# A hybrid decoder step on one core: another order of the attention units, and the first chunk of the next projection ahead of each attention's last value product

## The chip, the core and the metric

The kernel runs on one core of one Trainium2 chip. The metric is the device time of one execution in microseconds; the median of three runs is quoted. The profile is one further execution, recorded by the hardware profiler; its span runs from the first to the last recorded instruction.

## The reference, cut

One layer of a decoder trunk over 1024 prompt rows and 8 sample rows. Every group of heads gets its columns from one input projection; four groups are mixed, gated, projected back and added to the input.

```python
hn = rms_norm(x, g_n)
p = hn @ w_in                      # q, k, v, gates, pool input, z: 31 tiles of 128 columns
o_a = fox_attention(...)           # 4 heads, causal, cumulative log-forget bias
o_b = nsa_attention(...)           # gate0*compressed + gate1*selected blocks + gate2*sliding window
o_c = pool_mix(...)                # trailing means, one linear map for each channel group
o_m = mem_attention(q, mem_kv)     # 4 heads into 256 memory tokens
y = x + (concat(o_a, o_b, o_c, o_m) * silu(z)) @ w_out
y = rms_norm(y, final_g)
...
```

Each attention is a masked softmax of scores times values. The 8 sample rows read their past keys and values from paged caches; `cache_nsa_kv` is one of them.

## The kernel before, in words

**Projections.** The weights are taken in 31 tiles of 128 columns (TILES). A tile is multiplied in three chunks of 344 rows, and a chunk is 8 blocks of the contraction by 3 passes (high by high, low by high, high by low parts; lines 551 to 553, in `passes`), 24 matmuls. `project(m)` does the three chunks of tile m, `chunk(n)` (L584) the single chunk n % 3 of tile n // 3, so chunk 27 is the first chunk of tile 9. POOL splits each weight tile into its two parts (`split`, L1982 and L1984), and SP loads it.

**Attention units.** All attention is cut into 56 units, `attention_units` (L80): what, the pair of heads j, the block i of 128 queries, the first block of keys and the number nk of key blocks of 128. Units 0 to 7 are the memory attention (nk 4), 8 to 23 FoX (FOX_0 = 8; nk = i + 1), 24 to 55 the selected and window branches of NSA (NSA_0 = 24). Before, FoX takes its units in pairs of both j with nk 4, 4, 8, 8, 7, 7, 6, 6, 5, 5, 3, 3, 2, 2, 1, 1; NSA four units of 4, then by falling length 8, 8, 7, 7, 6, 6, ten of 5, and four each of 3, 2 and 1. A unit is wide if nk > 4. WIN_U is the first window unit of full length (5 blocks); there DVE makes the window table (L1548, L1549).

**One unit on the engines.** PE makes scores (`scores`, L667), DVE their negative maxima (`negmax`, L1507) and ACT the exponentials. PE turns the probabilities P by transposes (`turn_p`, L683, into three banks: the fourth piece waits until the first is copied out); ACT copies the even pieces (L1133) and DVE the odd ones (L1561). PE multiplies the turned P with the values (`weigh_v`, L704) and transposes the sums (L708), and DVE multiplies the result by the reciprocal sums into the output (`norm`, L1538 for memory and FoX, L1542 for NSA). In NSA, POOL adds the part to the output (L2071). For FoX, POOL adds the causal mask to the last block of the unit's forget table (L2056). The loop on PE is `attend(u0, u1)` (L711): for each u it issues scores(u), weigh_v(u - 2), turn_p(u - 1). weigh_v waits for the copies of that unit's turned P and for the multiply of the unit before (semaphore s_on). At its end, attend waits for s_on to reach u1, for the last multiply.

**The order of the work.** A list written by hand, STEPS (L109), sets one order of steps for PE, ACT and DVE. attend 0 is memory, attend 1 FoX, attend 2 NSA; behind each stand projection steps. `gates` (L804) are matmuls of 16 columns. `pair_job` (L741, step "pair") turns one pair of pages of `cache_nsa_kv`, which SP loads in its own order (`load_pair`, L2126, four transfers for a pair); from the thirteenth load on (q = 12, the first for pair 6) they stand behind

```python
if q == 12:
    sp.wait_ge(s_on, PHASE[0][1])    # 8: the last multiply of the memory attention
```

Of the kernel before, what the change touches and what calls it, by code (L numbers as in the profile page):

```python
# [79 lines left out]
def attention_units():  # L80

    mem = [("mem", j, i2, 0, 4) for i2 in range(NQ // 2) for j in range(2)]
    fox = [("fox", j, i, 0, i + 1) for i in (3, 7, 6, 5, 4, 2, 1, 0) for j in range(2)]
    nsa = [("sel", j, i, 0, i + 1) for i in range(NQ) for j in range(2)]
    nsa += [("win", j, i, max(0, i - WIN_T), min(i, WIN_T) + 1) for i in range(NQ) for j in range(2)]
    return mem, fox, sorted(nsa, key=lambda u: (u[4] != 4, -u[4]))


MEM_U, FOX_U, NSA_U = attention_units()
UNITS = MEM_U + FOX_U + NSA_U  # L90

WIN_U = next(u for u in range(len(UNITS)) if UNITS[u][0] == "win" and UNITS[u][2] >= WIN_T)
NSA_0 = len(MEM_U) + len(FOX_U)
# [7 lines left out]
def groups(u):  # L101
# [11 lines left out]
         ("project", 5), ("natural", 4), ("take", 5), ("project", 6), ("pair", 4), ("pair", 5), ("take", 6),  # L113
         ("project", 7), ("natural", 6), ("take", 7), ("first", 0), ("natural", 7), ("project", 8), ("take", 8),
         ("attend", 0),
         ("chunk", 27), ("gates", 0), ("pair", 6), ("chunk", 28), ("chunk", 29), ("take", 9),
         ("chunk", 30), ("natural", 9), ("forget", 0), ("forget", 1), ("chunk", 31), ("chunk", 32), ("take", 10),
         ("chunk", 33), ("natural", 10), ("chunk", 34), ("chunk", 35), ("take", 11),
         ("chunk", 36), ("first", 1), ("pair", 7), ("chunk", 37), ("chunk", 38), ("take", 12), ("attend", 1),
         ("project", 13), ("natural", 2), ("natural", 5), ("take", 13), ("gather", 0),  # L120
         ("project", 14), ("natural", 13), ("take", 14),
         ("project", 15), ("take", 15), ("compress", 0), ("pair", 8), ("pair", 9), ("gather", 1),
         ("project", 16), ("pair", 10), ("pair", 11), ("natural", 15), ("take", 16),
# [3 lines left out]
         ("project", 19), ("cmp_turn", 0), ("take", 19),  # L127
         ("chunk", 60), ("natural", 19), ("cmp_out", 0), ("chunk", 61), ("first", 2), ("cmp_out", 1), ("chunk", 62),
         ("take", 20), ("attend", 2),
         ("project", 21), ("natural", 20), ("take", 21), ("pool_mean", 0),  # L130
         ("project", 22), ("take", 22), ("pool_mean", 1),
         ("project", 23), ("pool_last", 0), ("pool_map", 0), ("take", 23),
         ("project", 24), ("take", 24), ("sample_new", 0),
# [38 lines left out]
def build(nc, x_p, x_s, c_fox, c_lf, c_nsa, st_win, st_pool, c_mem, ptab, mem_p, norm_g, w_in, b_f, pe_, w1,  # L172
# [3 lines left out]
    with ExitStack() as ctx:  # L176
# [328 lines left out]
        def _(pe):  # L505
# [140 lines left out]
            def scores(u):  # L646
                what, j, i, k0, nk = UNITS[u]
                done = u - 2 if nk <= 4 and u and UNITS[u - 1][4] <= 4 else u - 1
                if done >= 0 and UNITS[done][0] == "mem":
                    pe.wait_ge(s_P, 2 * (done + 1))  # L650
                elif done >= 0:
                    pe.wait_ge(s_nm, 2 * (done + 1))
                q, k = AUG[:, Q_AT[what] + j, :], AUG[:, K_AT[what] + j, :]
                if what == "mem":
                    for a in range(2):
                        for e in range(2):
                            r = slice(e * DH, (e + 1) * DH)
                            last = mm(bk(score_bank(u, e))[:, a * NMEM:(a + 1) * NMEM],
                                      q[r, (2 * i + a) * P:(2 * i + a + 1) * P], k[r, 0:NMEM], start=True, stop=True)
                    last.then_inc(s_S, 1)  # L660
                    return
                masks = {nk - 1: m_diag} if what == "fox" and i == 3 else {}
                parts = [(c, min(4, nk - c), e) for c in range(0, nk, 4) for e in range(2)]
                inside = {c: [b for b in masks if c <= b < c + 4] for c in range(0, nk, 4)}
                for c, n, e in parts:
                    r = slice(e * DH, (e + 1) * DH)
                    last = mm(bk(score_bank(u, e) + c // 4)[:, 0:n * P], q[r, i * P:(i + 1) * P],  # L667
                              k[r, (k0 + c) * P:(k0 + c + n) * P], start=True, stop=not inside[c])
                for c, n, e in parts:
                    for b in inside[c]:  # L670
                        last = mm(bk(score_bank(u, e) + c // 4)[:, (b - c) * P:(b - c + 1) * P], identb[:, :],
                                  masks[b][:, :], start=False, stop=(b == inside[c][-1]))
                last.then_inc(s_S, 1)
# [12 lines left out]
            def weigh_v(u):  # L686
                what, j, i, k0, nk = UNITS[u]
                pe.wait_ge(s_cA, even(G0[u + 1]))
                pe.wait_ge(s_cD, odd(G0[u + 1]))
                if u:  # L690
                    pe.wait_ge(s_on, u)
                wide = 2 if what == "mem" else 1
                for b in range(2 if what == "mem" else nk):
                    for e in range(2):
                        h, t = 2 * j + e, k0 + b
                        v = {"fox": nat[:, t, 256 + h * DH:256 + (h + 1) * DH],
                             "mem": nat[:, t, 256 + h * DH:256 + (h + 1) * DH],
                             "sel": nat[:, t, 384 + j * DH:384 + (j + 1) * DH],
                             "win": vw[:, t, j * DH:(j + 1) * DH]}[what]
                        if what == "mem":  # L700
                            p_ = turned_p(u, e, 0, 4).rearrange("p (a t c) -> p t a c", a=2, t=2)[:, b]
                        else:
                            p_ = turned_p(u, e, b, 1)
                        mm(bk(7)[e * DH:(e + 1) * DH, 0:wide * P], v, p_, start=(b == 0),  # L704
                           stop=(b == (1 if what == "mem" else nk - 1)))
                pe.wait_ge(s_rb, u + 1)
                for a in range(wide):
                    last = tr(bk(7)[:, (2 + a) * P:(3 + a) * P], sums_at(u)[0][:, a * P:(a + 1) * P], ident[:, :])  # L708
                last.then_inc(s_pv, 1)

            def attend(u0, u1):  # L711

                jobs_taken()
                turn_p(u0)
                if u0 == 0:
                    taken(8)
                elif u0 == FOX_0:
                    taken(12)
                scores(u0 + 1)
                if u0 == NSA_0:  # L720
                    taken(20)
                for u in range(u0 + 2, u1 + 2):
                    if u < u1:
                        scores(u)
                    weigh_v(u - 2)
                    if u - 1 < u1:
                        turn_p(u - 1)

                pe.wait_ge(s_on, u1)
                pe.wait_ge(s_cA, even(G0[u1]))  # L730
                pe.wait_ge(s_cD, odd(G0[u1]))
# [1229 lines left out]
        def _(pool):  # L1961
# [84 lines left out]
            pool.wait_ge(s_aug, 64)  # L2046
            for u in range(FOX_0 + 2, NSA_0):
                _, j, i, _, _ = UNITS[u]
                if u == FOX_0 + 4:
                    pool.wait_ge(s_proj, 13)  # L2050
                    split(0, 16 * 8, WH[:, 0, :, :], WL[:, 0, :, :], 15)
                if u >= FOX_0 + 4:
                    pool.wait_ge(s_nm, 2 * (u - 1))
                for e in range(2):
                    last_block = FORGET[2 * j + e][:, i * P:(i + 1) * P]
                    g.tensor_tensor(last_block, last_block, m_diag[:, :], ALU.add).then_inc(s_fm, 1)  # L2056
# [345 lines left out]
```

## Time and profile before

| what | us |
|---|---|
| median of three runs | 820.71 (818.95 to 821.31) |
| the profiled execution | 821.78 |
| its span | 820.0 |
| PE busy | 768.3 (94%) |
| VectorE (DVE) busy | 378.9 (46%) |
| ScalarE (ACT) busy | 282.2 (34%) |
| GpSimd (POOL) busy | 170.3 (21%) |

The rows below come from the profiled execution. A page part counts the whole span. A timeline lists one engine's instructions in order, runs of equal ones as one row with their count; what stands in brackets is the time that the engine idled ahead of the row, and the instruction that ended it. A windows view gives busy time inside a stretch, and the clock granted to TensorE as a share of full speed. PEld is the weight load of TensorE, SPq is SP's DMA queue. Some matmuls in f32 count twice in the trace: the four value products of a memory unit stand there as x8.

### The profile page before, as it was taken

To read this page: it belongs to the slowest core of one execution; us is meant where nothing else is said; L and a number is where in the kernel's file an instruction comes from. 1 tells how busy PE (TensorE), PEld (TensorE's weight loads), DVE (VectorE), ACT (ScalarE), POOL (GpSimd) and SP (SyncE) were. 2 spreads that over 40 slices of the span, in tenths; PEclk is the share of its full clock that TensorE was granted. 3 is DMA by queue.
4 is the path that set the end of the run, shared out by engine and by line. 5 is a ranking of instruction groups with operands and counts; after the bars stand their busy time and mean duration, and the time that the engine had idled before them with its cause. 6 is when DMAs were issued, how large, how long until landed. Compare 5 with 4: busy or idle time off the path is not lost.

```text
span 820.0 us, 15201 instructions
## 1 busy us (share of the span) xinstructions
PE 768.3 (94%) x5664; PEld 644.7 (79%) x5664; DVE 378.9 (46%) x828; ACT 282.2 (34%) x638; POOL 170.3 (21%) x164
## 2 busy tenths in 40 slices
PE   2999998998998999999989999899999999999996
PEld 2899866996777999999857776599988888777773
DVE  4742363425762301313467877738731126624334
ACT  6522363223672202311246766502122225312111
POOL 4146640242120420320220111225222220000000
PEclk9999999999999999999999999999999999999999
DMA  8523300353303455121500000003425567465621
GB/s 269 145 72 98 80 2 14 70 155 106 155 1 120 151 144 169 51 69 46 168 3 2 2 1 2 2 18 79 116 75 163 174 199 217 142 207 172 183 81 55
DMA packets 101880, 81.52 MB, mean 99 GB/s; under 512 B 10013, under 2 KB 95276, under 8 KB 101736
## 3 DMA queue, kind: packets, MB, share of 16 engines
q1 hardware_dynamic: 100352, 79.74, 32.2%
q10 hardware_dynamic: 1456, 0.82, 0.5%
q8 instruction: 45, 0.74, 0.4%
q14 instruction: 27, 0.22, 0.1%
HBM read 70.91 MB, written 13.87 MB: 103 GB/s over the span
## 4 chain that ended last, share of the span: by engine, by line
PE 81%; DVE 5%; SPq 4%; issue 4%; ACT 3%; DMA 2%; POOL 2%; POOLq 0%; DVEq 0%; ACTq 0%
PE PS L551 15%; PE PS L553 15%; PE PS L552 15%; PE PS L704 7%; PE PS L683 6%; PE PS L667 5%; PE PS L767 4%; PE PS L899 2%; SPq L2126 2%; PE PS L987 2%; PE PS L708 2%; SPq L2109 1%; DMA OB<-in_x_prompt 1%; POOL WL L1984 1%; PE PS L741 1%
## 5 line engine op out<-in xcount | busy, mean ns | idle before, releaser
L551 PE MATMUL PS<-HH,WH 128*128 128x344 f32 (+1 forms) x752 | 258.6, 344 | 6.8 <-issue 1.8
L553 PE MATMUL PS<-HH,WL 128*128 128x344 f32 (+1 forms) x752 | 252.7, 336 | 0.0
L552 PE MATMUL PS<-HL,WH 128*128 128x344 f32 (+1 forms) x752 | 252.6, 336 | 0.0
L551 PEld LDWEIGHTS PS<-HH,WH 128*128 128x128 f32 x752 | 143.8, 191 | 20.0 <-issue 7.0
L552 PEld LDWEIGHTS PS<-HL,WH 128*128 128x128 f32 x752 | 143.9, 191 | 5.9 <-issue 0.5
L553 PEld LDWEIGHTS PS<-HH,WL 128*128 128x128 f32 x752 | 143.8, 191 | 5.7
L1982 POOL TENSOR_TENSOR WH<-WR,onesc 128x1024 fp32r<-128x1024 f32 x31 | 60.9, 1965 | 343.8 <-PE PS L553 215.5
L1240 ACT ACTIVATE PP<-PP,stat 128x640 f32<-128x640 f32 (+7 forms) x96 | 70.8, 739 | 31.3 <-DVE stat L1507 31.3
L1984 POOL TENSOR_TENSOR WL<-WR,WH 128x1024 fp32r<-128x1024 f32 x31 | 76.6, 2471 | 2.4
L683 PE MATMUL PS<-ident,PP 128*128 128x128 f32 x472 | 65.6, 278 | 2.5 <-ACT AUG L1133 0.8
L667 PE MATMUL PS<-AUG 64*128 64x512 f32 (+3 forms) x288 | 57.6, 505 | 3.7 <-DVE stat L1507 2.0
L1561 DVE COPY AUG<-PS 128x256 f32<-128x256 f32 (+3 forms) x80 | 41.9, 524 | 40.9 <-PE PS L683 40.5
L683 PEld LDWEIGHTS PS<-ident,PP 128*128 128x128 f32 x472 | 53.7, 142 | 7.3 <-ACT AUG L1133 5.3
L704 PE MATMUL PS<-AUG,NAT 128*64 128x128 f32 (+1 forms) x640 | 47.2, 289 | 8.9 <-DVE OB L1538 5.1
L704 PEld LDWEIGHTS PS<-AUG,NAT 128*64 128x64 f32 x640 | 35.7, 136 | 24.8 <-ACT AUG L1133 13.3
L1133 ACT ACTIVATE AUG<-PS 128x384 f32<-128x384 f32 (+4 forms) x88 | 47.1, 539 | 5.4 <-PE PS L683 4.0
L1133 ACT ACTIVATE NAT<-PS 128x512 f32<-128x512 f32 (+1 forms) x37 | 20.8, 563 | 75.2 <-PE PS L643 27.0
L667 PEld LDWEIGHTS PS<-AUG 64*128 64x128 f32 x288 | 24.0, 187 | 24.2 <-issue 18.6
L1386 ACT ACTIVATE WR<-PP 128x1024 f32<-128x1024 f32 (+1 forms) x9 | 9.5, 1058 | 87.1 <-DVE PP L1949 79.9
L1822 DVE COPY NAT<-PS 128x512 f32<-128x512 f32 x16 | 11.1, 692 | 57.8 <-PE PS L899 57.6
L2071 POOL TENSOR_TENSOR OB<-OB,XT 128x128 f32<-128x128 f32 x32 | 14.5, 454 | 101.0 <-DVE XT L1542 101.0
L767 PE MATMUL PS<-OB,PP 128*128 128x161 f32 x256 | 35.5, 300 | 0.0
(346 smaller groups left out, 969.2 us busy)
## 6 DMA issues: line engine op xcount, KB each, us to landing
WR<-in_w_in SPq DMA_DIRECT2D x26, 512.0 KB, 5.3
PP<-in_nsa_w SPq DMA_DIRECT2D x16, 512.0 KB, 4.5
OB<-in_x_prompt SPq DMA_DIRECT2D x8, 512.0 KB, 6.6
out<-NAT SPq DMA_DIRECT2D x2, 2048.0 KB, 7.7
PP<-in_cache_fox_kv SPq DMA_DIRECT2D x32, 128.0 KB, 2.2
WR<-in_x_prompt SPq DMA_DIRECT2D x8, 512.0 KB, 4.1
out<-PP SPq DMA_DIRECT2D x8, 512.0 KB, 2.9
out<-in_state_nsa_win SPq DMA_DIRECT2D x1, 4088.0 KB
```

Source lines behind the costliest of these rows:

```text
L551: mm(out, lhs[0], rhs[0], start=(k == 0), stop=False)
L552: mm(out, lhs[0], rhs[1], start=False, stop=False)
L553: return mm(out, lhs[1], rhs[0], start=False, stop=(k == KC - 1))
L667: last = mm(bk(score_bank(u, e) + c // 4)[:, 0:n * P], q[r, i * P:(i + 1) * P], k[r, (k0 + c) * P:(k0 + c + n) * P], start=True, stop=not ...
L683: last = tr(bk(4 + g % 3)[:, (b - c) * P:(b - c + 1) * P], PP[:, p0:p0 + P], ident[:, :])
L704: mm(bk(7)[e * DH:(e + 1) * DH, 0:wide * P], v, p_, start=(b == 0), stop=(b == (1 if what == "mem" else nk - 1)))
L767: last = mm(bk(3 * kind + e)[:, 0:R_ALL + 1], w1s[:, n % 4, jj, e * P:(e + 1) * P], FT[:, j, :], start=(j == 0), stop=(j == NJ - 1))
L1133: return act1(out, in_, ACT.Copy)
L1240: last = act1(PP[:, c:c + nk * P], PP[:, c:c + nk * P], ACT.Exp, bias=stat[:, k:k + 1], scale=-1.0, accum_out=stat[:, 16 + k:17 + k])
L1561: v.tensor_copy(turned_p(u - 1, e, c, n), bk(4 + g % 3)[:, 0:n * P]).then_inc(s_cD, 1)
L1982: g.tensor_tensor(hi_, WR[:, s, :, :], ones, ALU.mult).then_inc(s_wcp, 1)
L1984: g.tensor_tensor(lo_, WR[:, s, :, :], hi_.bitcast(F32), ALU.subtract).then_inc(s_split, 1)
```

## The change

Three edits. (1) `attention_units` gives another order. FoX goes nk 4, 4, 8, 7, 6, 8, 5, 7, 3, 6, 2, 5, 1, 3, 2, 1. NSA keeps four units of 4 ahead, then goes in triples of two wide units and one short one (8, 8, 2; 7, 7, 2; 6, 6, 2; 5, 5, 2; and four of 5, 5, 1), and ends with the four units of 3. WIN_U moves from unit 36 to 40. (2) The first chunk of tiles 9, 13 and 21 leaves STEPS and is issued by PE inside attend, between the last unit's transposes and its value product. (3) POOL's wait ahead of a FoX mask is worked out from the last unit of the same pair of heads, since pairs no longer alternate.

```diff
--- before.py
+++ after.py
@@ -80,10 +80,15 @@
 def attention_units():
 
     mem = [("mem", j, i2, 0, 4) for i2 in range(NQ // 2) for j in range(2)]
-    fox = [("fox", j, i, 0, i + 1) for i in (3, 7, 6, 5, 4, 2, 1, 0) for j in range(2)]
+    fox = [("fox", j, i, 0, i + 1) for j, i in
+           ((0, 3), (1, 3), (0, 7), (0, 6), (0, 5), (1, 7), (0, 4), (1, 6), (0, 2), (1, 5), (0, 1), (1, 4), (0, 0),
+            (1, 2), (1, 1), (1, 0))]
     nsa = [("sel", j, i, 0, i + 1) for i in range(NQ) for j in range(2)]
     nsa += [("win", j, i, max(0, i - WIN_T), min(i, WIN_T) + 1) for i in range(NQ) for j in range(2)]
-    return mem, fox, sorted(nsa, key=lambda u: (u[4] != 4, -u[4]))
+    nsa = sorted(nsa, key=lambda u: -u[4])
+    middle, long_, short = ([u for u in nsa if u[4] in s] for s in ((3, 4), (5, 6, 7, 8), (1, 2)))
+    mixed = [u for n in range(8) for u in (long_[2 * n], long_[2 * n + 1], short[n])]
+    return mem, fox, middle[:4] + mixed + middle[4:]
 
 
 MEM_U, FOX_U, NSA_U = attention_units()
@@ -113,11 +118,11 @@
          ("project", 5), ("natural", 4), ("take", 5), ("project", 6), ("pair", 4), ("pair", 5), ("take", 6),
          ("project", 7), ("natural", 6), ("take", 7), ("first", 0), ("natural", 7), ("project", 8), ("take", 8),
          ("attend", 0),
-         ("chunk", 27), ("gates", 0), ("pair", 6), ("chunk", 28), ("chunk", 29), ("take", 9),
+         ("gates", 0), ("pair", 6), ("chunk", 28), ("chunk", 29), ("take", 9),
          ("chunk", 30), ("natural", 9), ("forget", 0), ("forget", 1), ("chunk", 31), ("chunk", 32), ("take", 10),
          ("chunk", 33), ("natural", 10), ("chunk", 34), ("chunk", 35), ("take", 11),
          ("chunk", 36), ("first", 1), ("pair", 7), ("chunk", 37), ("chunk", 38), ("take", 12), ("attend", 1),
-         ("project", 13), ("natural", 2), ("natural", 5), ("take", 13), ("gather", 0),
+         ("chunk", 40), ("chunk", 41), ("natural", 2), ("natural", 5), ("take", 13), ("gather", 0),
          ("project", 14), ("natural", 13), ("take", 14),
          ("project", 15), ("take", 15), ("compress", 0), ("pair", 8), ("pair", 9), ("gather", 1),
          ("project", 16), ("pair", 10), ("pair", 11), ("natural", 15), ("take", 16),
@@ -127,7 +132,7 @@
          ("project", 19), ("cmp_turn", 0), ("take", 19),
          ("chunk", 60), ("natural", 19), ("cmp_out", 0), ("chunk", 61), ("first", 2), ("cmp_out", 1), ("chunk", 62),
          ("take", 20), ("attend", 2),
-         ("project", 21), ("natural", 20), ("take", 21), ("pool_mean", 0),
+         ("chunk", 64), ("chunk", 65), ("natural", 20), ("take", 21), ("pool_mean", 0),
          ("project", 22), ("take", 22), ("pool_mean", 1),
          ("project", 23), ("pool_last", 0), ("pool_map", 0), ("take", 23),
          ("project", 24), ("take", 24), ("sample_new", 0),
@@ -722,6 +727,8 @@
                 for u in range(u0 + 2, u1 + 2):
                     if u < u1:
                         scores(u)
+                    if u == u1 + 1:
+                        chunk({len(MEM_U): 9, NSA_0: 13, len(UNITS): 21}[u1], 0)
                     weigh_v(u - 2)
                     if u - 1 < u1:
                         turn_p(u - 1)
@@ -2046,11 +2053,12 @@
             pool.wait_ge(s_aug, 64)
             for u in range(FOX_0 + 2, NSA_0):
                 _, j, i, _, _ = UNITS[u]
+                previous = max(w for w in range(FOX_0, u) if UNITS[w][1] == j)
                 if u == FOX_0 + 4:
                     pool.wait_ge(s_proj, 13)
                     split(0, 16 * 8, WH[:, 0, :, :], WL[:, 0, :, :], 15)
-                if u >= FOX_0 + 4:
-                    pool.wait_ge(s_nm, 2 * (u - 1))
+                if previous >= FOX_0 + 2:
+                    pool.wait_ge(s_nm, 2 * (previous + 1))
                 for e in range(2):
                     last_block = FORGET[2 * j + e][:, i * P:(i + 1) * P]
                     g.tensor_tensor(last_block, last_block, m_diag[:, :], ALU.add).then_inc(s_fm, 1)
```

Three places where the order on an engine differs.

PE at the end of memory attention: the last unit's transposes (ident, PP), its value product (AUG, NAT) and the transposes of its sums, chunk 27 (HH, WH; HL, WH; HH, WL, eight times), the gates (GS, XT) and pair 6 (64x128 from PP). Before:

```order
L683 MATMUL PS<-ident,PP 128x128 x8
L704 MATMUL PS<-AUG,NAT 64x256 x4
L708 MATMUL PS<-ident,KW 128x128 x2
L551 MATMUL PS<-HH,WH 128x344
L552 MATMUL PS<-HL,WH 128x344
L553 MATMUL PS<-HH,WL 128x344
...
L804 MATMUL PS<-GS,XT 128x16 x8
L804 MATMUL PS<-GS,XT 8x16
L741 MATMUL PS<-ident,PP 64x128 x8
```

and after, where the same functions stand five to seven lines lower in the file:

```order
L688 MATMUL PS<-ident,PP 128x128 x8
L556 MATMUL PS<-HH,WH 128x344
L557 MATMUL PS<-HL,WH 128x344
L558 MATMUL PS<-HH,WL 128x344
...
L709 MATMUL PS<-AUG,NAT 64x256 x4
L713 MATMUL PS<-ident,KW 128x128 x2
L811 MATMUL PS<-GS,XT 128x16 x8
L811 MATMUL PS<-GS,XT 8x16
L748 MATMUL PS<-ident,PP 64x128 x8
```

Chunk 27 stands ahead of the last value product, and between that product and pair 6 only the gates are left.

PE in NSA, among the 5-block units: transposes (ident, PP), scores (AUG alone; 512 and 128 columns make 5 blocks), value product (AUG, VW) and the transpose of the sums (ident, XT). Before, one 5-block unit after another:

```order
L683 MATMUL PS<-ident,PP 128x128 x10
L667 MATMUL PS<-AUG 128x512 x2
L667 MATMUL PS<-AUG 128x128 x2
L704 MATMUL PS<-AUG,VW 64x128 x10
L708 MATMUL PS<-ident,XT 128x128
L683 MATMUL PS<-ident,PP 128x128 x10
```

and after:

```order
L688 MATMUL PS<-ident,PP 128x128 x10
L672 MATMUL PS<-AUG 128x128 x2
L709 MATMUL PS<-AUG,VW 64x128 x10
L713 MATMUL PS<-ident,XT 128x128
L688 MATMUL PS<-ident,PP 128x128 x10
L672 MATMUL PS<-AUG 128x512 x2
L672 MATMUL PS<-AUG 128x128 x2
L709 MATMUL PS<-AUG,VW 64x128 x10
L713 MATMUL PS<-ident,XT 128x128
L688 MATMUL PS<-ident,PP 128x128 x2
```

Ahead of the value product of a long unit now stand the scores of a one-block unit (128 columns alone), and behind it come the long unit's transposes or the short unit's two.

POOL in FoX: the adds of the mask (m_diag) to the forget tables, and the split of the weights of tile 14 (WH and WL). Before:

```order
L2056 TENSOR_TENSOR AUG<-AUG,m_diag 128x128 x2
L2056 TENSOR_TENSOR VW<-VW,m_diag 128x128
L2056 TENSOR_TENSOR XT<-XT,m_diag 128x128
L1982 TENSOR_TENSOR WH<-WR,onesc 128x1024
L1984 TENSOR_TENSOR WL<-WR,WH 128x1024
L2056 TENSOR_TENSOR AUG<-AUG,m_diag 128x128 x2
```

and after:

```order
L2064 TENSOR_TENSOR AUG<-AUG,m_diag 128x128 x4
L1989 TENSOR_TENSOR WH<-WR,onesc 128x1024
L1991 TENSOR_TENSOR WL<-WR,WH 128x1024
L2064 TENSOR_TENSOR AUG<-AUG,m_diag 128x128 x2
L2064 TENSOR_TENSOR VW<-VW,m_diag 128x128
L2064 TENSOR_TENSOR XT<-XT,m_diag 128x128
```

The split keeps its place in the count of units, but the mask ahead of it belongs to unit 11, of the same pair of heads as unit 10.

## Rows read from the trace of the kernel before

**Rows 1.** Page part 1: busy us, share of the span and instructions of each engine.

```profile
PE 768.3 (94%) x5664; PEld 644.7 (79%) x5664; DVE 378.9 (46%) x828; ACT 282.2 (34%) x638; POOL 170.3 (21%) x164
```

**Rows 2.** Timeline of PE, end of memory attention: start, duration, instruction [idle before <-releaser].

```profile
132.05 1.04 PE L683 MATMUL PS<-ident,PP 128*128 128x128 f32 x8
134.29 1.08 PE L704 MATMUL PS<-AUG,NAT 128*64 128x256 f32 x8 [1.21 <-DVE OB L1538]
...
136.68 0.49 PE L551 MATMUL PS<-HH,WH 128*128 128x344 f32 x1 [0.93 <-DVE OB L1538]
...
142.19 2.09 PE L804 MATMUL PS<-GS,XT 48*128 48x16 f32 x18
144.21 1.09 PE L741 MATMUL PS<-ident,PP 128*64 128x128 f32 x16
```

**Rows 3.** Windows: stretch, length, busy PE, PEld, DVE, ACT, POOL, clock, DMA, GB/s.

```profile
137.00:140.00 3.00, 3.00 (x12) 3.00 (x12) 0.00 (x0) 0.00 (x0) 0.00 (x0) 0.50 0.09 22
...
257.00:259.00 2.00, 2.00 (x9) 2.00 (x8) 0.00 (x0) 0.00 (x0) 0.00 (x0) 0.50 0.87 233
...
533.00:536.00 3.00, 3.00 (x13) 3.00 (x11) 0.00 (x0) 0.00 (x0) 0.00 (x0) 0.50 0.00 0
416.83:420.24 3.41, 1.35 (x17) 1.02 (x17) 3.34 (x10) 1.51 (x5) 0.25 (x1) 1.00 0.01 4
421.00:423.00 2.00, 2.00 (x8) 1.37 (x9) 0.76 (x3) 1.30 (x4) 0.00 (x0) 0.50 0.01 2
```

**Rows 4.** Windows, line 551 alone, chunks 28 and 29: busy PE, PEld, clock, DMA, GB/s.

```profile
145.24:152.80 7.56, 5.22 (x16) 3.05 (x17) 1.00 0.37 59
```

**Rows 5.** Timeline of SP's queue: the issues of the loads from pair 6 on.

```profile
137.37 10.06 SPq L2126 DMA_DIRECT2D PP<-in_cache_nsa_kv  x8
```

**Rows 6.** DMA issues, 130 to 150 us: count, KB each, median us to landing.

```profile
PP<-in_cache_nsa_kv SPq DMA_DIRECT2D x8, 64.0 KB, 2.3
```

**Rows 7.** Timeline of PE, the short units of FoX.

```profile
239.45 0.44 PE L683 MATMUL PS<-ident,PP 128*128 128x128 f32 x2 [0.21 <-ACT AUG L1133]
...
243.86 0.88 PE L704 MATMUL PS<-AUG,NAT 128*64 128x128 f32 x12 [0.30 <-DVE OB L1538]
...
248.97 0.66 PE L704 MATMUL PS<-AUG,NAT 128*64 128x128 f32 x8 [0.38 <-DVE OB L1538]
...
254.52 0.44 PE L704 MATMUL PS<-AUG,NAT 128*64 128x128 f32 x4 [0.67 <-DVE OB L1538]
```

**Rows 8.** Timeline of PE, NSA: 5-block units, then the step to a short one.

```profile
491.70 1.31 PE L704 MATMUL PS<-AUG,VW 128*64 128x128 f32 x20
...
493.11 1.51 PE L683 MATMUL PS<-ident,PP 128*128 128x128 f32 x10
...
502.62 0.44 PE L683 MATMUL PS<-ident,PP 128*128 128x128 f32 x2 [0.63 <-ACT AUG L1133]
```

**Rows 9.** Groups of PE, 503 to 533 us: count, busy, mean ns, idle before, releaser.

```profile
L704 PE MATMUL PS<-AUG,VW 128*64 128x128 f32 x68 | 5.3, 280 | 2.7 <-DVE XT L1542 2.7
...
L704 PE MATMUL PS<-AUG,NAT 128*64 128x128 f32 x48 | 3.9, 282 | 1.1 <-DVE XT L1542 0.9
```

**Rows 10.** Timeline of DVE, NSA: the window table and the first minimum behind it.

```profile
466.98 0.81 DVE L1548 COPY NAT<-OB 128x640 f32<-128x640 f32 x1
...
468.16 0.82 DVE L1507 CUSTOM_DVE_ANT_1 PP<-PS,NAT 128x640 f32<-128x640 f32 x1
```

**Rows 11.** Timelines of DVE and POOL: a small multiply beside a POOL add, and alone.

```profile
491.26 0.45 DVE L1527 TENSOR_TENSOR stat<-stat,fga 128x2 f32<-128x2 f32 x1
...
505.60 0.16 DVE L1527 TENSOR_TENSOR stat<-stat,fga 128x2 f32<-128x2 f32 x1
...
491.23 0.45 POOL L2071 TENSOR_TENSOR OB<-OB,XT 128x128 f32<-128x128 f32 x1 [3.67 <-DVE XT L1542]
```

**Rows 12.** Page part 5: the two halves of POOL's weight split.

```profile
L1982 POOL TENSOR_TENSOR WH<-WR,onesc 128x1024 fp32r<-128x1024 f32 x31 | 60.9, 1965 | 343.8 <-PE PS L553 215.5
...
L1984 POOL TENSOR_TENSOR WL<-WR,WH 128x1024 fp32r<-128x1024 f32 x31 | 76.6, 2471 | 2.4
```

## The prediction

> **What bounds the kernel now.** I read the page's first part, then PE's own timeline at the three places the change touches, then the rows of the engines that release PE there. PE is busy for 768.3 of 820.0 us [rows 1], so only 52 us without PE work exist, and a change that adds, drops or resizes no matmul can win only idle PE time or time at the lower clock. Near each attention's end both occur. In memory attention PE idles 1.21 us before the last unit's value product and 0.93 us before chunk 27 [rows 2]; the short units of FoX idle 0.30 to 0.67 us each, those of NSA 3.8 together [rows 7, 9]. Right after each end the granted clock is 0.50, which is 1.2 of 2.4 GHz, while PE is busy for the whole stretch: 137 to 140, 257 to 259, 533 to 536 us [rows 3]. Two chunks at the full clock take 7.56 us, so one takes 3.8 [rows 4]; chunk 27, begun just before the clock fell, took 5.5 (136.68 to 142.19, [rows 2]). A fall at an end thus costs 1.7 us; it follows the idle tail of the attention. The same happens after 416.83 to 420.24, where PE worked 1.35 us of 3.41.
>
> **The change part by part.** All sums are against the profiled execution, 821.78 us (span 820.0), which lies 1.07 above the median of the three runs, 820.71.
>
> *Memory end: chunk 27 first.* Before, the last transposes start at 132.05 and their eight are issued by about 133.0; chunk 28 starts at 145.24, 12.2 us later [rows 2, 4]. After: chunk 27 fills the 1.2 us gap and runs at the full clock, 133.0 to 136.8. The value product and the wait behind it take what they take now, 134.29 to 136.68 = 2.4 us, so the attention is over at 139.2. Then the gate matmuls, 2.0 us (142.19 to 144.21), to 141.2. Next stands pair 6, and here the cover has gone. Its four DMAs are queued on SP behind the same end of the attention: today PE, which waits for the last multiply, goes on at 136.68 [rows 2], SP issues the first of eight at 137.37 and all in 10.06 us [rows 5], so one per 1.36 us (7 steps and one issue taken as 0.54), the fourth at 141.45; with 2.3 us to land [rows 6] it is there at 143.75, 7.1 us after the multiply. Today chunk 27 and the gates stand in those 7.1 us, and pair 6 starts at 144.21 with 0.45 us to spare. In the new order only the gates do: the data lands at 139.1 + 7.1 = 146.2, PE waits 5.0 us from 141.2, pair 6 takes 1.0 (144.21 to 145.24), and chunk 28 starts at 147.3, that is 2.0 us later than now although the fall at 137 is gone. And the wait itself is a stretch with less PE work than 416.83 to 420.24 has, after which the clock fell [rows 3]: 1.7 more for chunks 28 and 29. Together **+3.7 us**; bounds +2.0 (no fall) and +4.6 (pair 6 and what follows at half speed for longer). Later loads of that SP queue (o_lf, w 11 and on) shift with it and keep their distance to PE.
>
> *FoX and NSA ends.* The chunk fills the wait before the last value product (counted below) and keeps PE busy, so the falls at 257 and 533 should go: **-1.7 us each**. The waits behind the last value product stay. Chunks 39 and 63 are covered by splits that are done long before. The next loads (w1 for compress, state rows behind natural 20) are needed tens of us later, or stand behind the same PE step as now.
>
> *FoX order.* PE's work is the same; only waits change. A value product waits for the DVE copy of that unit's turned P and the multiply of the unit before; what covers this is only the score matmul of the unit two ahead. That gives the prices: 0.30 with a copy of 3 blocks and scores of 2, 0.38 with 2 and 1, 0.67 with 1 and no scores [rows 7]. Before, FoX has 0.30 twice, 0.38 twice, 0.67 twice: 2.70. New: unit 16 (3 blocks, then scores of 2) 0.30; 18 (2, then 1) 0.38; 20 (1, then 2) about 0; 21 (3, then 1) between 0.38 and 0.67, taken 0.5; 22 (2, no scores) above 0.67, taken 0.8; 23 hidden by the chunk. Sum 2.0: a gain of 0.7. Against it: when a short unit follows a long one, ACT takes the short unit's exponentials before the copies of the long one's turned P, and PE's fourth transposed piece waits for them: 0.21 at 239.45 [rows 7], 0.63 at 502.62 in NSA [rows 8]. Once before, three times now (units 15, 17, 19): 3 x 0.45 less 0.21 = +1.1. And the long units 17 and 19 find less cover for their own exponentials: the rows show none of this, so 0 to 0.63 each, taken 0.4: +0.8. FoX order: **+1.2 us**.
>
> *NSA order.* The twelve waits before value products of the short units sum to 3.8 (2.7 and 1.1, [rows 9]). They move rather than vanish: the value product of the long unit ahead of a short one now has only the short scores as cover. A 5-block unit's last copy is 2 blocks, so with scores of 1 block it pays 0.38, as the 2-block unit did [rows 7]: four times 1.5; the four with scores of 2 blocks 0.43, 0.30, 0.30, 0.17; the closing 3-block units 0.06, 0.06, and 0.9 with no scores: 3.8 again. The 0.63 goes, but eight long-to-short steps pay 0 to 0.2 each, taken 0.08: together 0. In the four triples of 5, 5 and 1 blocks PE comes to the long units' scores and transposes about 0.1 to 0.3 us early: +0.8. One more: the window table is made on DVE (466.98 to 468.16 = 1.2) ahead of the first 5-block window unit [rows 10], whose two minima of 0.82 then take 1.6. Before, PE had 1.3 of value product and 1.5 of transposes (491.70 and 493.11, [rows 8]) as cover; now the unit ahead has 2 blocks, four of those ten transposes, 0.6: +0.9. NSA order: **+1.7 us**.
>
> *POOL's order in FoX.* Units 10 and 11 share head pair 0, so mask 11 waits for unit 10, and the split for tile 14 stands behind it, beside units 10 to 12, not before them. It is 2.0 and 2.5 us [rows 12]; mask 12 comes behind it, about when its scores end: 0. Its other price is DVE: a tiny multiply with both inputs in SBUF took 0.45 beside a POOL add against 0.16 alone [rows 11], so a long POOL instruction could hold one for 2.5. Between copies and minima, DVE has such a step once per unit, just before and just after the split: taken 0, bound 2.5. The Trainium skill (SBUF — State Buffer, Who interferes with whom) says that such a DVE step and a POOL instruction exclude each other for the whole instruction, the later one blocking. The 0.45 agrees. By that rule alone, with both halves hit, this part would cost 4.5 us at most.
>
> Sum: +3.7 - 1.7 + 1.2 - 1.7 + 1.7 = **+3.2 us**; 820.71 + 3.2 = 823.9 for the median.
>
> **The rivals.** (1) *The change does what its words say*: the short units' waits vanish between the long ones. That wins 2.9 in FoX (2.70 and 0.21) and 4.4 in NSA (3.8 and 0.63), with the two falls 3.4; with the +3.7 of the memory end still paid, 820.71 - 7.0 = 813.7. For it: the long units show hardly a wait today. Against: a value product's cover is the scores of the unit two ahead, and that gets shorter for the long units. (2) *Pair 6 does not hold PE*: if its data came within the 2.0 us of the gates, chunk 28 would start at 142.3, 2.9 us earlier than now: 820.71 + 3.2 - 6.6 = 817.3, faster. It decides on whether SP issues four loads in under 2 us; rows 5 show 1.36 per load. (3) *The falls stay*: the tails still idle enough that the clock falls under the next chunks, at one end or both, or in a new place: +1.7 to +3.4, 827.3 at both. For it: the last three FoX units and the last NSA unit but one still idle 0.5 to 0.9 us. (4) *The split blocks DVE* in FoX: 823.9 + 2.5 to 4.5 at most, 828.
>
> **How the numbers follow.** My forecast, the wait for pair 6 with the falls at the two later ends gone, 0.58. Rival 1 0.12, rival 2 0.10, rival 3 0.15, rival 4 0.05. The likeliest gives **823.9 us**. The range leaves out rival 1 and the far end of rival 4: 817.3 (rival 2) to 828.0 (rivals 3 and 4). Within the forecast alone the terms' bounds give 821.5 to 826. About 0.3%, 2.5 us, is what a measurement tells from no change. Faster by more: rival 1 and most of rival 2, 0.19. Within: the lower quarter of the forecast and the rest of rival 2, 0.18. Slower: the remaining forecast and rivals 3 and 4, 0.63.
>
> **What would show it.** PE idle of about 5 us before the pair 6 matmuls, released by a DMA, followed by a granted clock of 0.50; no fall right at the ends of FoX and NSA; idle rows of about 0.38 before the value products of 5-block units ahead of a short one; an NSA phase no shorter apart from the clock. I am wrong if pair 6 starts right behind the gates, or if both phases are shorter by several us with the clock at 1.00 in both runs.

## The result, and the profile after

The changed kernel takes **826.96 us** (median of 8 executions, 825.43 to 830.22) against 821.01 for the kernel before in the same job (8 executions, 817.15 to 824.79). The ratio is 1.0058, 95% interval 1.0038 to 1.0077: slower by 0.6%. The forecast was 823.9 us, slower, range 817.3 to 828.0. The profiled execution took 826.87 us, with a span of 825.1, so the two traces stand 5.1 us apart.

Page part 1 after the change [rows 1]:

```profile
PE 769.7 (93%) x5664; PEld 644.8 (78%) x5664; DVE 380.2 (46%) x828; ACT 281.3 (34%) x638; POOL 170.8 (21%) x164
```

PE's count of matmuls is the same; its busy time rose by 1.4 us, and the rest of the 5.1 is idle time. A stretch in which the granted clock stands at half is called a fall below. The timeline of PE at the end of memory attention (columns as in [rows 2]):

```profile
130.71 1.08 PE L709 MATMUL PS<-AUG,NAT 128*64 128x256 f32 x8 [1.21 <-DVE OB L1545]
...
132.80 0.40 PE L556 MATMUL PS<-HH,WH 128*128 128x344 f32 x1
...
136.75 1.08 PE L709 MATMUL PS<-AUG,NAT 128*64 128x256 f32 x8
...
139.13 2.09 PE L811 MATMUL PS<-GS,XT 48*128 48x16 f32 x18 [0.93 <-DVE OB L1545]
146.09 1.98 PE L748 MATMUL PS<-ident,PP 128*64 128x128 f32 x16 [4.87 <-DMA PP<-in_cache_nsa_kv]
148.00 0.66 PE L556 MATMUL PS<-HH,WH 128*128 128x344 f32 x1
```

Chunk 27 fills one of the two gaps of 1.21 us and runs at the full clock, as meant. Behind the gates PE now waits 4.87 us for pair 6's data, then works at half speed: the pair takes 1.98 us where it took 1.09, and chunk 28 goes on at the slow clock.

The windows view of the changed kernel (columns as in [rows 3]):

```profile
143.00:146.00 3.00, 0.00 (x0) 0.00 (x0) 1.64 (x5) 1.22 (x2) 0.00 (x0) 0.50 0.15 44
148.00:151.50 3.50, 3.50 (x14) 3.50 (x13) 0.00 (x0) 1.10 (x1) 0.00 (x0) 0.50 0.28 59
260.00:263.00 3.00, 3.00 (x21) 3.00 (x20) 0.49 (x2) 0.29 (x2) 0.00 (x0) 1.00 0.00 0
384.00:390.00 6.00, 6.00 (x51) 5.32 (x50) 3.86 (x8) 1.12 (x2) 0.00 (x0) 0.50 0.01 3
539.70:543.00 3.30, 3.30 (x28) 2.74 (x26) 0.00 (x0) 0.00 (x0) 0.00 (x0) 1.00 0.00 0
```

The clock is at half through the wait and the first half of chunk 28. It stays at 1.00 through the chunks at the ends of FoX (260 to 263) and NSA (539.7 to 543), and no fall comes behind these ends, where [rows 3] had 0.50. And it is at half in a place that had no fall before: 384 to 390 us, from the last of the compressed scores on.

The short units, timeline of PE in FoX [rows 7]:

```profile
234.94 0.55 PE L688 MATMUL PS<-ident,PP 128*128 128x128 f32 x3 [0.42 <-ACT AUG L1140]
...
243.17 0.55 PE L688 MATMUL PS<-ident,PP 128*128 128x128 f32 x3 [0.32 <-ACT AUG L1140]
...
249.02 1.09 PE L688 MATMUL PS<-ident,PP 128*128 128x128 f32 x8 [0.15 <-ACT PP L1247]
...
258.89 0.66 PE L709 MATMUL PS<-AUG,NAT 128*64 128x128 f32 x8 [0.80 <-DVE OB L1545]
...
265.11 0.43 PE L556 MATMUL PS<-HH,WH 128*128 128x344 f32 x1 [0.69 <-DVE OB L1545]
```

and in NSA [rows 8, 9]:

```profile
486.78 1.35 PE L672 MATMUL PS<-AUG 64*128 64x512 f32 x8 [0.97 <-DVE stat L1514]
...
491.13 1.31 PE L709 MATMUL PS<-AUG,VW 128*64 128x128 f32 x20 [0.38 <-DVE XT L1549]
...
501.35 1.31 PE L709 MATMUL PS<-AUG,VW 128*64 128x128 f32 x20 [0.39 <-DVE XT L1549]
...
536.38 0.88 PE L709 MATMUL PS<-AUG,VW 128*64 128x128 f32 x12 [0.94 <-DVE XT L1549]
...
543.70 0.43 PE L556 MATMUL PS<-HH,WH 128*128 128x344 f32 x1 [0.69 <-DVE XT L1549]
```

The waits moved to other rows: in NSA, the window table's wait (0.97), those of the 5-block units ahead of a one-block unit (0.38, four times) and the closing one (0.94) are new.

Cut at the same instructions, the two traces differ as follows (each figure the distance of two starts on PE; the last two columns are further executions of the same kernels, below):

| stretch | before | change | differs | before again | change again |
|---|---|---|---|---|---|
| unit 6's value product to FoX's first waiting scores | 63.00 | 67.56 | +4.56 | 64.01, 63.96 | 67.03, 67.23 |
| from there to natural 2 (FoX, its end, tile 13) | 76.50 | 75.88 | -0.62 | 76.52, 76.50 | 75.90, 75.91 |
| to NSA's first waiting scores | 145.23 | 148.24 | +3.01 | 145.23, 145.23 | 148.28, 148.25 |
| to the sample's first scores (NSA, its end, tile 21) | 168.47 | 167.83 | -0.64 | 168.44, 168.44 | 167.30, 169.06 |
| to the first matmul of W_out | 113.64 | 112.46 | -1.18 | 113.45, 113.62 | 111.96, 113.46 |

Outside these the two profiled traces agree within 0.1 us. The stretch to the sample's first scores also holds the fall at NSA's start, which [rows 3] show at 421 to 423 us: from NSA's first waiting scores to the row of 0.32 behind them PE takes 15.07 us before and 14.16 in the change, where this fall comes later in the stretch (425 to 428.4).

### The profile page after: what moved, and what is told of

The parts are those of the page before. It is cut to its first block, busy times and chain, and to the rows that moved or that the text cites. A ratio compares the mean times of both kernels' runs of the same rounds, so it can differ in the third digit from the quotient of the medians.

```text
span 825.1 us, 15198 instructions
## 1 busy us (share of the span) xinstructions
PE 769.7 (93%) x5664; PEld 644.8 (78%) x5664; DVE 380.2 (46%) x828; ACT 281.3 (34%) x638; POOL 170.8 (21%) x164
## 4 chain that ended last, share of the span: by engine, by line
PE 84%; DVE 4%; ACT 4%; issue 3%; DMA 1%; POOL 1%; SPq 1%; DVEq 0%; POOLq 0%; ACTq 0%
PE PS L556 17%; PE PS L558 16%; PE PS L557 16%; PE PS L709 6%; PE PS L672 5%; PE PS L688 5%; PE PS L774 4%; PE PS L906 2%; PE PS L994 2%; PE PS L713 1%; ACT PP L1247 1%; PE PS L748 1%; DMA OB<-in_x_prompt 1%; PE PS L550 1%; DVE PP L1514 1%
```

## The experiments

What was expected of each experiment stands ahead of what was measured. The theory at this point: the memory end costs 4.6 us since pair 6's loads lost their cover; the unit orders cost a little, the chunk ahead gains a little at FoX and NSA; the rest is falls elsewhere. Each kernel ran beside the kernel before; the medians of before were 822.34 us (30 executions, first four runs), 822.88 (17, the next) and 823.18 (9, the last).

**Chunk 27 put back** (the other two chunks and both orders stay):

```diff
-                    if u == u1 + 1:
-                        chunk({len(MEM_U): 9, NSA_0: 13, len(UNITS): 21}[u1], 0)
+                    if u == u1 + 1 and u1 != len(MEM_U):
+                        chunk({NSA_0: 13, len(UNITS): 21}[u1], 0)
...
-         ("gates", 0), ("pair", 6), ("chunk", 28), ("chunk", 29), ("take", 9),
+         ("chunk", 27), ("gates", 0), ("pair", 6), ("chunk", 28), ("chunk", 29), ("take", 9),
```

> The change with its first chunk undone: chunk 27 stands behind the memory attention again, the two other chunks and both unit orders stay. Theory (pair 6's loads lost their cover): PE no longer idles before pair 6 (4.87 us in the changed kernel; below 0.5 here), chunk 28 starts near 145.2 as before the change, and FoX starts 4.6 us sooner than in the changed kernel, so about 826.96 - 4.6 = 822.4 us. Rival (the new unit orders cost the time): it stays at 825 or more. Rival (the fall of the clock at 384 to 390 us belongs to the change): that fall is still there, 825.

Measured: 822.17 us, ratio 1.000 (0.998 to 1.002). The memory stretch takes 62.46 us, 5.1 less than in the change, and no fall comes at the compressed scores. Timeline of PE:

```profile
140.81 2.09 PE L811 MATMUL PS<-GS,XT 48*128 48x16 f32 x18
143.85 1.09 PE L748 MATMUL PS<-ident,PP 128*64 128x128 f32 x16 [0.95 <-DMA PP<-in_cache_nsa_kv]
```

So the rival that the orders carry the whole loss is out. The wait of 0.95 is the one detail missed (expected below 0.5): chunk 27 ran at the full clock here, and then even it and the gates don't cover the loads. The next kernels with this order at the memory end wait likewise: 0.90 us with the orders alone, 0.97 and 0.92 in two further executions of the kernel before.

**Pair 6 behind chunks 28 and 29**, on the changed kernel:

```diff
-         ("gates", 0), ("pair", 6), ("chunk", 28), ("chunk", 29), ("take", 9),
+         ("gates", 0), ("chunk", 28), ("chunk", 29), ("pair", 6), ("take", 9),
```

> The changed kernel with pair 6 moved behind chunks 28 and 29; the chunk ahead stays everywhere. Theory (only the place of pair 6 costs): the value product ends near 138.2, the gates near 141.2, chunks 28 and 29 take 7.6 (9.3 if the clock falls), pair 6 finds its data and does not wait, chunk 30 starts near 150 where it started at 152.8 before the change: 4.6 + 3 us less than the changed kernel, about 819.4 us (821 with a fall). Rival (the chunk ahead itself costs, by the later value product and what waits for it): no better than 825.

Measured: 821.11 us, ratio 0.998 (0.997 to 1.000). Pair 6 starts without a wait (one of its sixteen records is missing from the trace):

```profile
152.18 1.09 PE L748 MATMUL PS<-ident,PP 128*64 128x128 f32 x15
```

The memory stretch takes 61.72 us, 5.8 less than in the change, with a fall at 143 to 147 us. That is the value expected with a fall. The chunk ahead itself costs nothing at this end; what stood behind it did.

**The orders alone**, no chunk ahead:

```diff
-                    if u == u1 + 1:
-                        chunk({len(MEM_U): 9, NSA_0: 13, len(UNITS): 21}[u1], 0)
...
-         ("gates", 0), ("pair", 6), ("chunk", 28), ("chunk", 29), ("take", 9),
+         ("chunk", 27), ("gates", 0), ("pair", 6), ("chunk", 28), ("chunk", 29), ("take", 9),
...
-         ("chunk", 40), ("chunk", 41), ("natural", 2)
+         ("project", 13), ("natural", 2)
...
-         ("chunk", 64), ("chunk", 65), ("natural", 20)
+         ("project", 21), ("natural", 20)
```

> The kernel before with both new unit orders (and POOL's wait that goes with them), no chunk ahead. Theory (the orders move the waits about): idle PE time in FoX and NSA together 0 to 2 us more than before, the clock falls at the ends stay, 821.0 + 1 = 822 us. Rival (the orders do what their words say): 7 us less, 814. Rival (the orders carry the loss): 825 or more.

Measured: 823.71 us, ratio 1.003 (1.000 to 1.006): neither a gain of 7 us nor the whole loss. Timeline of PE, the first scores with DVE's wait in FoX and in NSA, and the first matmul behind each attention:

```profile
199.31 1.99 PE L672 MATMUL PS<-AUG 64*128 64x512 f32 x8 [1.40 <-DVE stat L1512]
...
260.38 0.42 PE L556 MATMUL PS<-HH,WH 128*128 128x344 f32 x1 [0.69 <-DVE OB L1543]
...
433.55 1.99 PE L672 MATMUL PS<-AUG 64*128 64x512 f32 x8 [0.32 <-DVE stat L1512]
...
537.93 0.43 PE L556 MATMUL PS<-HH,WH 128*128 128x344 f32 x1 [0.69 <-DVE XT L1547]
```

Between these rows lie 61.07 and 104.38 us; between the same rows of before (196.51 to 255.91 and 430.56 to 532.12) 59.40 and 101.56. No fall lies inside in either kernel. So the orders cost 1.67 in FoX and 2.82 in NSA, 4.5 together. Only 1.4 shows in the medians. In the profiled execution the clock did not fall at either end, where it fell in all three of before; that gave back 1.5 us behind FoX and 1.6 behind NSA, and 4.5 - 3.1 is 1.4. This is one trace: three of the twelve executions took 830.65 to 831.49 at a mean clock of 0.981, the others 821.54 to 825.62, and which falls each had isn't known.

**The chunk ahead with the orders of before**, pair 6 behind chunk 29:

```diff
-    fox = [("fox", j, i, 0, i + 1) for j, i in
...
+    fox = [("fox", j, i, 0, i + 1) for i in (3, 7, 6, 5, 4, 2, 1, 0) for j in range(2)]
...
+    return mem, fox, sorted(nsa, key=lambda u: (u[4] != 4, -u[4]))
...
-         ("gates", 0), ("pair", 6), ("chunk", 28), ("chunk", 29), ("take", 9),
+         ("gates", 0), ("chunk", 28), ("chunk", 29), ("pair", 6), ("take", 9),
```

> The unit orders of before, the chunk ahead of the last values at all three ends, and pair 6 behind chunks 28 and 29. Theory: 3.0 us less at the memory end than before the change, about 1 us less at each of the two other ends (no fall of the clock there), 821.0 - 5 = 816 us. Rival (the new orders are worth something): slower than the same with the new orders. Rival (the chunk ahead costs): 821 or more.

Measured: **817.12 us**, ratio 0.9935 (0.991 to 0.996), faster than before and 4.0 us below the same with the new orders. From the row of 0.32 in NSA to the first matmul behind it, 104.60 us: 3.04 more than before for a chunk that takes 3.78 at the full clock (half of [rows 4]). In FoX this execution had a fall in a new place (194.8 to 198.2 us); the kernel with the gates between the chunks, further down, has none there and takes 62.47 against 59.40, 3.07 more. A chunk ahead of the last value product gains 0.7 us at each of these ends, beside the fall that doesn't come.

**Page numbers read early**, on the changed kernel:

```diff
                 if q == 12:
+                    early.extend(page(NPG * n + k) for k in range(4))
                     sp.wait_ge(s_on, PHASE[0][1])
...
-                    pg = page(NPG * n + 2 * half + a)
+                    pg = early[2 * half + a] if q in (12, 13) else page(NPG * n + 2 * half + a)
```

> The changed kernel; on SP the four page numbers of pair 6 are read into registers before the wait for the end of the memory attention, not one ahead of each load behind it. Nothing else moves. Theory (what PE waits for is SP's queue, 1.36 us for each load, of which the read of the page number is the greater part): the four loads are issued at about 0.55 us each, the data of pair 6 lands some 2.4 us sooner, PE's 4.87 us wait shrinks to about 2.4, and FoX starts 2.4 us sooner or more (the stretch at half clock shrinks too): about 824 us. Rival (the landing of the data, not its issue, takes the time): the wait stays above 4 us and the time at 826 to 827.

Measured: 824.63 us, ratio 1.0022 (1.0005 to 1.0040); the change had 1.0058. SP's queue in the change, then here:

```profile
139.82 10.06 SPq L2134 DMA_DIRECT2D PP<-in_cache_nsa_kv  x8
```

```profile
139.39 8.34 SPq L2137 DMA_DIRECT2D PP<-in_cache_nsa_kv  x8
```

and PE here:

```profile
139.27 2.18 PE L811 MATMUL PS<-GS,XT 48*128 48x16 f32 x18 [0.93 <-DVE OB L1545]
143.93 1.98 PE L748 MATMUL PS<-ident,PP 128*64 128x128 f32 x16 [2.49 <-DMA PP<-in_cache_nsa_kv]
```

The wait is 2.49 us (2.4 expected), and the memory stretch 64.39, 3.2 less than in the change. What shrank is SP's issue: each of the four loads still lands 2.2 to 2.4 us behind its own issue in both traces. The price was split wrongly in the expectation. The first issue comes 0.57 us sooner behind the gates' start (0.12 against 0.69), and the eight take 1.72 less for three reads, so a read of a page number costs 0.57. The first four issues stand 0.73 us apart without it and 1.31 with it (the 1.36 is the mean over eight), so the issue itself costs 0.73, not 0.55.

**The gates between the chunks**, orders of before:

```diff
-         ("gates", 0), ("chunk", 28), ("chunk", 29), ("pair", 6), ("take", 9),
+         ("chunk", 28), ("gates", 0), ("chunk", 29), ("pair", 6), ("take", 9),
```

> The unit orders of before, the chunk ahead at all three ends, and behind the memory attention chunk 28, then the gates, chunk 29 and pair 6. Theory (a fall of the clock follows stretches in which PE has little to do; the run with the gates first had one at 140 to 144 us, behind 0.93 us of waiting and 2.0 us of gate matmuls): with chunk 28 between the wait and the gates that fall goes in most executions, 1.7 us less than with the gates first, about 815.5 us. Rival (the gates have nothing to do with it): the same 817 us.

Measured: **815.79 us**, ratio 0.9928 (0.990 to 0.995), the fastest of the study; the interval doesn't tell it from the 0.9935 with the gates first. Windows view, from chunk 28 to pair 6:

```profile
139.10:149.00 9.90, 9.90 (x66) 9.47 (x66) 1.64 (x8) 1.93 (x4) 0.00 (x0) 1.00 0.14 41
```

In this execution no fall comes at the memory end, and the stretch takes 60.38 us where the gates first took 61.63. Whether that holds in most executions isn't shown; the mean clock of the six (0.9915, against 0.9889 over the seven with the gates first) leans that way.

**The kernel before, twice more**, unchanged.

> The kernel before, once more, for its falls of the clock. Theory (a fall behind an attention's end or the compressed scores is a matter of the execution): the stretches at half clock are not those of the first execution, whose five were at 136.5, 256, 420, 532.5 and 683 us. Rival (they belong to the code): the same five stretches.

> The same as the look before it, a third execution of the kernel before: whether the falls at the ends of FoX and NSA come again.

Measured: 822.92 and 822.73 us. Both have falls at FoX's end (257 us), at NSA's start (421), at NSA's end (534) and at 684, as the first execution had. The fifth moved: in both it comes at 145 us, in chunk 28, not at 137. So chunk 27 ran at the full clock, and the timeline of PE of the first shows a wait that the prediction's trace didn't have:

```profile
140.96 2.09 PE L804 MATMUL PS<-GS,XT 48*128 48x16 f32 x18
144.02 1.09 PE L741 MATMUL PS<-ident,PP 128*64 128x128 f32 x16 [0.97 <-DMA PP<-in_cache_nsa_kv]
```

The theory that a fall at an attention's end is a matter of the execution is out for FoX and NSA: there it came six times in six. At the memory end its place did change.

**The changed kernel, twice more**, unchanged, and **with 1.9 us more work behind FoX** (results overwritten by the chunk that follows):

```diff
+                if (m, c) == (13, 1):
+                    for k in range(12):
+                        mm(bk(3 * s + c)[:, 0:CH], WH[:, s, k % KC, :], hh[:, k % KC, t], start=True, stop=True)
```

> The changed kernel once more, for its falls of the clock. Theory (the two ends of FoX and NSA are cured by the chunk; the falls in untouched stretches depend on when the stretch runs, which hardly differs between executions): the wait for pair 6 is 4.9 us again with a fall in it, no fall at the ends of FoX and NSA, the fall behind the compressed scores (384 to 391 us) is there again and none at 683. Rival (that fall is chance): it is not there, or another is at 683.

> The same as the look before it, a third execution of the changed kernel.

> The changed kernel with 12 more matmuls of the kind of a chunk (1.9 us at the full clock) right behind the end of FoX, whose results the chunk that follows overwrites: all that comes later runs 1.9 us later and is the same otherwise. Theory (whether the clock falls in the untouched stretches depends on when they run): the fall behind the compressed scores is gone, 3.0 us less against 1.9 us more, and 825.9 us in all, with a fall in another place perhaps. Rival (the fall follows what the change does in the stretches before): it stays, and the time is 826.96 + 1.9 = 828.9.

Measured: 826.79 and 828.68 us, and 828.69 for the kernel with more work (ratio 1.0071, 1.0046 to 1.0097). The wait for pair 6 with half clock in it is there in all three (4.42, 4.80 and 4.90 us), no fall at the ends of FoX and NSA in any. The fall at the compressed scores is there in all three too, also with the added work, where it was expected to go. But this was a weak test of the timing: the memory stretch took 66.36 us in that trace, so the compressed scores began at 382.11, against 380.96, 381.86 and 380.53 in the three executions of the change, which is 0.3 to 1.6 us later and not 1.9. That the fall depends on when the stretch runs is neither shown nor excluded. The fall at NSA's start varies from one execution of the change to the next: it lasts 3.4 us in the first, is absent in the second and lasts 6.8 us in the third. Timeline of PE at the compressed scores, in the change:

```profile
380.96 4.26 PE L832 MATMUL PS<-KCa,AUG 64*128 64x16 f32 x64
385.15 1.97 PE L648 MATMUL PS<-ident,XT 128*128 128x128 f32 x8
```

and before:

```profile
377.06 3.75 PE L825 MATMUL PS<-KCa,AUG 64*128 64x16 f32 x64
380.74 1.09 PE L643 MATMUL PS<-ident,XT 128*128 128x128 f32 x8
```

The instructions and their neighbours are the same, and PE has no idle row there in either. The eight transposes take 1.97 us against 1.09.

## Why the prediction was right, and where it was off

The sign and the cause were right. In the table's stretches for the three priced places, the profiled pair has 4.56 - 0.62 - 0.64 = **+3.3 us against +3.2**. That this meets so closely is partly luck. The memory end was 0.9 over its price, and the -0.64 holds 0.9 that no term priced, the fall at NSA's start; without it, NSA's order and end come to +0.3. Over three executions of each kernel the memory end is 67.27 - 63.66 = +3.6, FoX -0.6, NSA's order and end +0.3: +3.3 again, now place by place near the forecast's 3.7, -0.5 and 0.0.

The median came out 3.1 us above the forecast, and above the 821.5 to 826 that the forecast's own terms allowed; it lies inside the range because the range reached up to rivals 3 and 4. The excess has two parts. Falls in stretches that the change doesn't touch add 1.4 us over three executions of each kernel (+3.0 at the compressed scores, -0.7 at NSA's start, -0.9 ahead of W_out). The rest, some 1.6, is of the size by which the kernel before was faster beside the first measurement of the change (821.01) than beside the experiments (822.34 to 823.18). Over all executions the means are 822.6 and 827.2, 4.7 apart.

- **Memory end, +3.7: measured +4.56, +3.6 over three executions each.** The wait was forecast as 5.0 us and is 4.87; chunk 28 was to start at 147.3 and starts at 148.00. What was missed is pair 6 itself at half speed (1.98 against 1.09); the bound of +4.6 named it. The 0.45 us to spare before the change was read from a trace in which chunk 27 ran at half clock; in the two further executions pair 6 waits 0.97 and 0.92 us, and the stretch takes 64.0, not 63.0. The chain behind it (one load per 1.36 us on SP, the gates as the only cover) is shown twice: by the reads moved ahead of the wait, and by pair 6 moved behind the chunks.
- **FoX order, +1.2: measured +0.9** (from the row of 1.40 to the matmul behind the attention 64.09, less a chunk of 3.78, less 59.40). The waits listed in the trace rose by only 0.4. Value products fell from 2.70 to 2.22, with the closing ones (0.52 and 0.80) as priced. The transposes that wait for ACT (0.42, 0.32, 0.21) rose by 0.7, where 1.1 was taken, and the long units' own exponentials cost 0.15, where 0.8 was taken. Of the other 0.5, 0.2 is the chunk, which takes 3.94 between its neighbours; the rest stands in no idle row.
- **NSA order, +1.7: measured +1.8** (107.15 - 3.78 - 101.56). The window table's 0.97 was forecast as 0.9, the four 5-block waits as 0.38 each, the last as 0.9 (0.94). The sum is right in part by luck: the listed waits rose by only 1.2. The 0.8 for long units that come early stands in no row, and a wait of 0.48 before the last one-block unit's value product had no price.
- **The falls at the two ends, -1.7 each: gone, worth 1.5 each.** With the chunk ahead none came in nine executions at either end; without it six in six in the kernel before, and none in the one execution of the new orders without it. So for the orders of before the cure is shown; with the new ones it isn't shown to be needed.
- **POOL's split, 0 with a bound of 2.5: nothing seen.** In the change the split runs from 206.28 to 210.6; the negative maxima beside it take 1.09 us, as those of the same size at 227.49 do. What did take longer beside POOL is a copy of each unit's reciprocal sums. Where it starts together with a pair of mask adds it took 0.48 us instead of 0.23 to 0.24, in five units of FoX in the change and in three before; the one at 211.36, which started inside a row of such adds, took 0.24:

```profile
205.54 0.48 DVE L1535 COPY KW<-stat 128x128 f32<-128x128 f32 x1
...
207.31 1.09 DVE L1514 CUSTOM_DVE_ANT_0 PP<-PS,AUG 128x896 f32<-128x896 f32 x1 [0.49 <-PE PS L672]
...
211.36 0.24 DVE L1535 COPY KW<-stat 128x128 f32<-128x128 f32 x1
...
238.98 0.48 DVE L1535 COPY KW<-stat 128x128 f32<-128x128 f32 x1
```

  The Trainium skill (SBUF — State Buffer, Who interferes with whom) has DVE contend with GpSimd when DVE reads two inputs from SBUF or copies in a two-port mode, and not when it has at most one input in SBUF outside those modes. The maxima agree, with one of their two inputs in PSUM. The copies of 0.48 agree if they ran in such a mode, which no run shows; the one at 211.36, beside adds throughout, does not. In the profiled execution of the change no DVE step is held for a half of the split.
- **What no term held: the clock elsewhere.** The fall at the compressed scores adds 3.0 us in three executions of three, and was in none of three of before; the fall at 683 us went in two of three (1.2 us in the profiled pair). So a part of rival 3 came true: it had a fall in a new place at +1.7, and this one lasts twice as long. Neither the orders nor the chunk ahead bring it by themselves: it was absent, in one trace each, with chunk 27 put back, with pair 6 late, with the orders alone and with the page numbers early, while a shorter one (3.4 us) came just behind it in both kernels with the orders of before and pair 6 late. What decides it stays open.

Over 132 executions of nine kernels, 0.001 of mean granted clock goes with 0.6 us within a kernel. The means were 0.988 before and 0.985 for the change, so 1.8 us of the 4.7 go with the clock, and 2.9 remain at an equal one; part of the low clock in the change lies in PE's wait, where it costs nothing.

Rival 1 (the words of the change) and rival 2 (pair 6 holds nothing) are out: the orders alone cost 4.5 us between the rows, and pair 6 held PE.

## What to carry to other kernels

When work is moved out of a gap, list everything that waits for the same event as the gap's end, on every queue: here chunk 27 was also the cover of four loads released by the same multiply, and moving those loads' consumer two chunks later turned +0.6% into -0.2%, and into -0.7% with the old unit orders. Mixing long and short units moves the waits when the cover of a unit's last step is the work of a neighbour; count the cover on both sides of each pair before reordering. Where a chain is nearly tight in the one trace, look at a second execution: a slow neighbour can hide the wait, as chunk 27 at half clock did for pair 6.

## What was not expected of the hardware

Through a run of 32 matmuls of 16 columns (x64 in the trace), with PE busy throughout, the clock goes to half in the changed kernel each time (384 to 391 us, 3.0 us lost) and never in the kernel before, though the instructions and their neighbours are the same. The fall started 3.1, 2.4 and 2.5 us after the first of these matmuls in three executions of the change, so it isn't tied to one instruction. And SP needs 1.36 us on average for a load whose page number is read from SBUF, 0.57 of it for the read.
